# Three of seven products issued 512 columns wide, with the halves added on VectorE and v normalised on ScalarE

## The reference, cut to what matters

```python
def _spatial_gating_mixer(h, w_in, ln_g, ln_b, w_s, b_s, w_out):
    bsz, s, _ = h.shape
    proj = h @ w_in                                  # 1024 -> 3 x 2048
    z = proj[..., :E_WIDTH]
    uv = jax.nn.gelu(proj[..., E_WIDTH:], approximate=False)
    u, v = jnp.split(uv, 2, axis=-1)
    v = _layernorm(v, ln_g, ln_b)
    vc = v.reshape(bsz, s // CHUNK, CHUNK, SG_HEADS, SG_HEAD_DIM)
    sv = jnp.einsum('gpq,bnqge->bnpge', w_s, vc) + b_s.T[None, None, :, :, None]
    y = u * sv.reshape(bsz, s, E_WIDTH) * jax.nn.silu(z)
    return y @ w_out
```

## Time and profile before

| What | Value |
|---|---|
| median of 3 runs | 814.75 us |
| span of the profiled execution, first to last instruction | 812.9 us |
| PE busy | 803.3 us, 99% of the span |
| DVE busy | 649.2 us, 80% |
| ACT busy | 442.6 us, 54% |
| mean granted TensorE clock | 0.998 |
| u and z stage, from its first matmul to the first of the output product | 535.86 to 712.02 us |

### The profile page before, as it was taken

One profiled execution on the slowest core, in us unless ns is written; L12 is line 12 of the kernel. 1 busy time (PEld: TensorE's weight loads), 2 busy tenths in 40 slices (PEclk: granted clock), 3 DMA queues, 4 the chain that ended last, 5 costly groups with the idle time before them and its releaser, 6 DMA issues.

```text
span 812.9 us, 15224 instructions
## 1 busy us (share of the span) xinstructions
PE 803.3 (99%) x5614; PEld 752.5 (93%) x5614; DVE 649.2 (80%) x950; ACT 442.6 (54%) x624; POOL 50.9 (6%) x68
## 2 busy tenths in 40 slices
PE   9999999999999999999999999999999999999997
PEld 8779999999999999988889888899999999988896
DVE  5989999999999999898653787567888888897534
ACT  4575656565656666562332844446667677762220
POOL 1010000000000000000000000010000000000000
PEclk9999999999999999999999999999999999999999
DMA  9994566666565656587422162414555445487103
GB/s 350 366 245 131 153 185 179 184 177 190 171 196 166 202 164 198 171 315 288 160 79 79 61 250 98 134 21 143 148 155 148 125 140 148 136 303 265 52 1 104
DMA packets 39566, 137.85 MB, mean 170 GB/s; under 512 B 4336, under 2 KB 6512, under 8 KB 39536
## 3 DMA queue, kind: packets, MB, share of 16 engines
q1 hardware_dynamic: 31616, 110.64, 37.0%
q0 software_dynamic: 6912, 25.17, 16.4%
q10 hardware_dynamic: 1008, 1.66, 0.6%
HBM read 108.09 MB, written 4.19 MB: 138 GB/s over the span
## 4 chain that ended last, share of the span: by engine, by line
PE 94%; DVE 3%; issue 2%; ACT 0%; POOL 0%; POOLq 0%; DVEq 0%; ACTq 0%
PE pp L1190 11%; PE pp L1191 11%; PE pp L1192 11%; PE pp L1046 8%; PE pp L1048 7%; PE pp L1047 7%; PE p_aux L1190 7%; PE p_aux L1192 7%; PE p_aux L1191 7%; PE pp L1328 4%; PE pp L1326 4%; PE pp L1327 4%; PE p_aux L1400 2%; PE pp L1145 1%; PE pp L1062 1%
## 5 line engine op out<-in xcount | busy, mean ns | idle before, releaser
L1190 PE MATMUL pp<-h_hi,wh 128*128 128x256 f32 x280 | 79.3, 283 | 0.0
L1192 PE MATMUL pp<-h_hi,wl 128*128 128x256 f32 x280 | 79.2, 283 | 0.0
L1191 PE MATMUL pp<-h_lo,wh 128*128 128x256 f32 x280 | 79.2, 283 | 0.0
L1701 DVE TENSOR_TENSOR wl<-wt,wh 128x1024 fp32r<-128x1024 f32 x56 | 66.5, 1219 | 0.2 <-ACT wh L698 0.2
L698 ACT ACTIVATE wh<-wt 128x1024 fp32r<-128x1024 f32 x56 | 58.9, 1054 | 13.7 <-DVE wt L1682 7.6
L1190 PE MATMUL pp<-s_hi,wh 128*128 128x256 f32 x224 | 63.4, 283 | 0.0
L1191 PE MATMUL pp<-s_lo,wh 128*128 128x256 f32 x224 | 63.4, 283 | 0.0
L1192 PE MATMUL pp<-s_hi,wl 128*128 128x256 f32 x224 | 63.4, 283 | 0.0
L1192 PE MATMUL p_aux<-s_hi,wl 128*128 128x256 f32 x224 | 63.4, 283 | 0.0
L1191 PE MATMUL p_aux<-s_lo,wh 128*128 128x256 f32 x224 | 63.4, 283 | 0.0
L1190 PE MATMUL p_aux<-s_hi,wh 128*128 128x256 f32 x224 | 63.4, 283 | 0.0
(11 more groups left out here) (237 smaller groups left out, 2598.1 us busy)
## 6 DMA issues: line engine op xcount, KB each, us to landing
raw<-in_stream SPq DMA_DIRECT2D x144, 512.0 KB, 4.0
wl<-raw POOLq DMA_DIRECT2D x28, 512.0 KB, 4.5
raw_l<-in_stream SPq DMA_DIRECT2D x18, 512.0 KB, 4.6
raw_s<-in_stream SPq DMA_DIRECT2D x16, 512.0 KB, 13.6
wl_b<-raw POOLq DMA_DIRECT2D x16, 512.0 KB, 4.5
raw_m<-in_stream SPq DMA_DIRECT2D x14, 512.0 KB, 3.2
x_s<-in_xt SPq DMA_DIRECT2D x4, 512.0 KB, 6.0
w_lo_s<-raw POOLq DMA_DIRECT2D x4, 512.0 KB, 5.4
```

What stands on the lines that cost most here:

```text
L1190: pe.matmul(out, hi, hi_of(k), start=fresh and k == 0, stop=False, skip_group_check=not fresh)
L1191: pe.matmul(out, hi, lo_of(k), start=False, stop=False, skip_group_check=not fresh)
L1192: mm = pe.matmul(out, lo, hi_of(k), start=False, stop=k == 3, skip_group_check=not fresh)
L1701: dve.tensor_tensor(wl[par][:, part], wt[par][:, part], f32(wh[par][:, part]), ALU.subtract).then_inc(t_cut, 1)
```

## The change

In Q1, Q6 and Q7 of each group the high weights are multiplied by high and low data in one matmul of 512 columns: the high half goes to the left half of bank A, the low half to the right one. The low weights times high data stay a matmul of 256 columns into the left half. For that `s_hi` with `s_lo`, and `h_hi` with `h_lo`, become one tensor each, at the addresses they had. The two halves of the bank must now be added: ScalarE copies the left half as before, and VectorE then adds the right half to the copy (`add_p`), and only this addition counts `copied_b`, on which TensorE waits. The layer norm of v moves from VectorE (`tensor_scalar`) to ScalarE (`Identity` with a scale and a bias for each partition); VectorE makes `minus_mean` once for it. The lists of both engines are put in another order.

```diff
-                act.activation(pc_b[:, g, (0, 2, 1)[n], :], bank_a_b[g][:, 0:HALF], ACT.Copy).then_inc(copied_b, 1)
+                act.activation(pc_b[:, g, (0, 2, 1)[n], :], bank_a_b[g][:, 0:HALF], ACT.Copy).then_inc(half_copied_b, 1)
+
+            def normalise(i):
+                if isinstance(i, int) and i == 0:
+                    act.wait_ge(ln_ready, 1)
+                act.wait_ge(sv_done, 2 * i + FREE)
+                for st in range(NCH):
+                    ...
+                    act.activation(vn[:, :, at_st], src, ACT.Identity, scale=ln_rstd[:, st:st + 1],
+                                   bias=minus_mean[:, st:st + 1]).then_inc(vn_cut, 1)
@@ beside_u
                 hi_t_b(i, 1, 1)
+                normalise(i)
+                copy_p_b(i, 0, 2)
                 hi_b2_b(i, 1)
-                copy_p_b(i, 0, 2)
                 neg_b2_b(1)
                 if not isinstance(i, int) or i:
                     silu_z_b(i - 1)
@@ beside_z
                 copy_p_b(i, 1, 0)
                 cut_b11_b(i + 1, 0)
+                copy_p_b(i, 1, 1)
+                hi_b2_b(i + 1, 0)
+                neg_b2_b(0)
                 hi_t_b(i + 1, 0, 0)
-                copy_p_b(i, 1, 1)
                 hi_t_b(i + 1, 0, 1)
-                hi_b2_b(i + 1, 0)
                 copy_p_b(i, 1, 2)
-                neg_b2_b(0)
                 gelu_u(i)
@@ tensor
+            def wide_product(bank, at, width, par, both_of, fresh):
+                for k in range(4):
+                    hi, lo = (a[par][:, at + width * k:at + width * k + P] for a in (wh_b, wl_b))
+                    both = both_of(k)
+                    def high(start):
+                        return pe.matmul(bank.rearrange("p (a e) -> p a e", e=HALF), hi, both, start=start, stop=k == 3,
+                                         skip_group_check=True)
+                    if k == 0:
+                        high(fresh)
+                    mm = pe.matmul(bank[:, 0:HALF], lo, both[:, 0, :], start=False, stop=False, skip_group_check=True)
+                    if k:
+                        mm = high(False)
+                mm.then_inc(prod_b, 1)
@@ vector
+            dve.scalar_tensor_tensor(out=minus_mean[:, :], in0=mv[:, :, 0], scalar=-1.0, in1=ln_rstd[:, :],
+                                     op0=ALU.mult, op1=ALU.mult).then_inc(ln_ready, 1)
+            def add_p(i, g, n):
+                part = pc_b[:, g, (0, 2, 1)[n], :]
+                dve.wait_ge(half_copied_b, of_b(i, g, 3, n + 1))
+                dve.tensor_tensor(part, part, bank_a_b[g][:, halves[1]], ALU.add).then_inc(copied_b, 1)
@@ while_u
+                    t_sums_b(i, 1)
+                add_p(i, 0, 0)
                 if later:
-                    t_sums_b(i, 1)
                     b11_low_b(i, 1)
                     c_12_b(i - 1, 1)
-                    mixed(i - 1)
+                    mixed(i - 1, (i, 0, 1))
+                else:
+                    add_p(i, 0, 1)
                 t_low_b(i, 1, 0)
                 if later:
                     times_u(i - 1)
-                t_low_b(i, 1, 1)
+                add_p(i, 0, 2)
                 if later:
                     after(at[0])
                 c_22_b(i, 0)
-                normalise(i)
+                t_low_b(i, 1, 1)
@@ while_z
+                add_p(i, 1, 0)
                 c_first_b(i, 0)
+                c_12_b(i, 0)
+                add_p(i, 1, 1)
                 t_sums_b(i + 1, 0)
                 b11_low_b(i + 1, 0)
-                c_12_b(i, 0)
                 if not isinstance(i, int) or i > 0:
                     times_z(i - 1, at[0])
-                t_low_b(i + 1, 0, 0)
-                t_low_b(i + 1, 0, 1)
+                add_p(i, 1, 2)
                 ...
                 c_22_b(i, 1)
+                t_low_b(i + 1, 0, 0)
+                t_low_b(i + 1, 0, 1)
```

More of the change, by code:

```diff
@@ L175, in build @@
         wt = [at_kb(f"wt{par}", 28 * par + 14, [P, 2048]) for par in range(2)]
-        s_hi = at_kb("s_hi", 92, [P, 4, 4, HALF], F32R)
-        s_lo = at_kb("s_lo", 108, [P, 4, 4, HALF], F32R)
+        s_both = at_kb("s_both", 92, [P, 2, 4, 4, HALF], F32R)
+        s_hi, s_lo = (s_both[:, n, :, :, :] for n in range(2))
         s_f = at_kb("s_f", 108, [P, 4, 4, HALF])
@@ L203, in build @@
         term = at_kb("term", 196, [P, 2, P])
-        h_hi = at_kb("h_hi", 60, [P, KD, S], F32R)
-        h_lo = at_kb("h_lo", 76, [P, KD, S], F32R)
+        h_both = at_kb("h_both", 60, [P, 2, KD, S], F32R)
+        h_hi, h_lo = (h_both[:, n, :, :] for n in range(2))
         raw = at_kb("raw", 156, [P, RING, SLOT])
@@ L220, in build @@
         mv = sb("mv", [P, NCH, 2])
+        minus_mean = sb("minus_mean", [P, NCH])
         ident = sb("ident", [P, P])
@@ L285, in build @@
         b11_hi_b, b11_cut_b, b2_in_b = sem("b11_hi_b"), sem("b11_cut_b"), [sem(f"b2_in_b{g}") for g in range(2)]
+        ln_ready, half_copied_b = sem("ln_ready"), sem("half_copied_b")
         neg_b, lo_begun_b = sem("neg_b"), sem("lo_begun_b")
@@ L602, in _ @@
             act.sem_inc(copied, OFF)
-            act.sem_inc(copied_b, OFF)
             def cut_hi(w, slot, land, first=False, to=w_hi):
@@ L933, in copy_p_b @@
                 act.wait_ge(c_sum_b, of_b(i, g, 3, OFF - 3))
-                act.activation(pc_b[:, g, (0, 2, 1)[n], :], bank_a_b[g][:, 0:HALF], ACT.Copy).then_inc(copied_b, 1)
+                act.activation(pc_b[:, g, (0, 2, 1)[n], :], bank_a_b[g][:, 0:HALF], ACT.Copy).then_inc(half_copied_b, 1)
[4 more added lines that the diff above has]
+                for st in range(NCH):
+                    at_st = slice(P * st, P * (st + 1))
+                    src = y32[:, 2 * i:2 * i + 2, at_st] if isinstance(i, int) else y32[:, bass.ds(2 * i, 2), at_st]
+                    act.activation(vn[:, :, at_st], src, ACT.Identity, scale=ln_rstd[:, st:st + 1],
+                                   bias=minus_mean[:, st:st + 1]).then_inc(vn_cut, 1)
             def gelu_u(i):
@@ L1364, in uq1 @@
                 pe.wait_ge(copied_b, of_b(i, g, 3, OFF - 3))
-                product(bank_a_b[g][:, left], B_11, P, g, *own(0, 0), True, 1)
+                wide_product(bank_a_b[g][:, :], B_11, P, g, lambda k: h_both[:, :, k, left], True)
             def uq5(i, g):
@@ L1375, in uq6 @@
                 pe.wait_ge(copied_b, of_b(i, g, 3, OFF + 1))
-                product(bank_a_b[g][:, left], 1024, P, g, *summed(S2), False, 1)
+                wide_product(bank_a_b[g][:, :], 1024, P, g, lambda k: s_both[:, :, S2, k, :], False)
             def uq7(i, g):
                 pe.wait_ge(copied_b, of_b(i, g, 3, OFF + 2))
-                product(bank_a_b[g][:, left], 512, P, g, *summed(S3), False, 1)
+                wide_product(bank_a_b[g][:, :], 512, P, g, lambda k: s_both[:, :, S3, k, :], False)
             def uq2(i, g):
@@ L1441, in _ @@
             dve.sem_inc(c_sum_b, OFF)
+            dve.sem_inc(copied_b, OFF)
             at = [0]
@@ L2103, in _, with mixed @@
             after(step(dve.tensor_copy(ln_rstd[:, :], rstd[:, :])))
+            dve.scalar_tensor_tensor(out=minus_mean[:, :], in0=mv[:, :, 0], scalar=-1.0, in1=ln_rstd[:, :],
+                                     op0=ALU.mult, op1=ALU.mult).then_inc(ln_ready, 1)
             dve.wait_ge(bs_in, 16)
             dve.wait_ge(sv_used, 2)
[L2108 to L2116, removed]
+            def add_p(i, g, n):
+                part = pc_b[:, g, (0, 2, 1)[n], :]
+                dve.wait_ge(half_copied_b, of_b(i, g, 3, n + 1))
+                dve.tensor_tensor(part, part, bank_a_b[g][:, halves[1]], ALU.add).then_inc(copied_b, 1)
+            def mixed(i, between=None):
                 n = []
@@ L2132, in mixed @@
                                              op0=ALU.mult, op1=ALU.add).then_inc(sv_used, 1)
+                    if u == 0 and between is not None:
+                        add_p(*between)
             def times_u(i):
@@ L2184, in _ @@
             dve.sem_inc(x_updated, 1)
+            add_p(last, 1, 0)
             c_first_b(last, 0)
             c_12_b(last, 0)
+            add_p(last, 1, 1)
             times_z(last - 1, at[0])
@@ L2190, in _ @@
             y_low(PAIRS, PAIRS + 2)
+            add_p(last, 1, 2)
             dve.wait_ge(y_made_b, last)
```

## The result

The changed kernel takes 835.49 us (median of 5 runs, 835.15 to 835.91), the kernel before 814.78 (814.71 to 814.98 for the first three, up to 815.23 for all 5): ratio 1.0253, 95% interval 1.0241 to 1.0264, 20.7 us slower. The forecast was 833.7.

What follows compares the result with a forecast made beforehand. TensorE, 94% of the chain, was taken as the bound. Step 0's 4.2, seven steps' 13.5 and step 1's 0.3 give +18.0; with 1 for the clock, 812.9 becomes 831.9, plus 1.85 around it 833.7 us; range 828 to 840.

Steps and rivals of the forecast that it cites:

- TensorE's saving: Joining pairs of 256-column matmuls into 512 saves 0.0133 us a pair, 0.32 a step, 2.56 us over 192 pairs.
- Stall at Q6 of z: TensorE waits 1.97 us there in steps 1 to 7 for copy, then addition; 0.10 of it was there before.
- `hi_b2_b` 0.95: On ScalarE `hi_b2_b` now stands behind copy 3 of u, putting 0.95 us more in the chain to Q6 of z.
- the layer norm 0.40: Four `Identity` take 2.0 us against 1.65 us of room less 0.05, so ScalarE's copy 3 is 0.40 us late.
- `Identity` 0.50: Each layer-norm `Identity` of 256 columns on ScalarE takes 0.50 us start to start; four take 2.0 us.
- The addition's part: Ahead of Q6 of z, VectorE's `add_p` takes 0.42 us plus 0.04 for the gap after ScalarE's copy.
- Stall at Q6 of u: VectorE's list from Q6 of z reaches its addition late, so TensorE waits 0.38 us in each step.
- Step 1's extra 0.3: Step 1 waits another 0.3 us at Q6 of u, as its VectorE list starts late.
- Step 0: First `add_p` stands behind the layer-norm statistics on VectorE: TensorE stalls 4.07 us at Q6 of u; whole step +4.2.
- cheap layer norm: Rival: `Identity` costs like a copy and fits ScalarE's 1.65 us room; +14.4, 829.2 us, chance 0.15.
- extra table load: Rival: `Identity` isn't in gelu's table, adding 1.29 us to the chain in 7 steps; 842.8 us, chance 0.05.
- lower clock between the stalls of 2 us: Rival: each step's 2 us idle drops TensorE's clock, about 1 us a step more; 841 us, chance 0.08.

Runs made afterwards that it cites:

- the last two runs: Changed kernel with its queues reordered, 814.08 us; and the kernel before with only ScalarE's copy of Q1 of z ahead of table load and silus, 814.47 us.
- the run on the kernel before: The kernel before with one line moved: on ScalarE `hi_b2_b` behind the copy of Q7 of u instead of ahead of it; 821.54 us, ratio 1.0081.

## Why the prediction was right, point by point

By the profiled executions the difference is 833.3 - 812.9 = 20.4 us:

| part | forecast | measured |
|---|---|---|
| stage's start to mix 0 (step 0, clock) | 4.2 + 1 | 18.45 - 12.96 = 5.5 |
| mix 0 to mix 7 (7 periods) | 13.5 + 0.3 | 167.33 - 154.22 = 13.1 |
| behind mix 7, to the stage's end | 0 | 0.1 |
| before the stage | 0 | 1.0 |
| behind the stage | 0 | 0.7 |

- **TensorE's saving**: 0.053 us a product forecast, 0.04 measured. The sum took the price of a 512-wide matmul from a stream of its own kind; between 256-wide ones it stands about 0.235 from the next, not 0.227. So 1.9 us, not 2.56. The Trainium skill's 2.5 ns beyond the columns ("TensorE: Matmul & The Clock Gate", "Wait — 56ns, not 53.3ns?") would give, as an estimate, 24 x 2.5 = 60 ns a step. The 0.24 us between the last two runs is four times that, so the row was the better guide.
- **Stall at Q6 of z**: 1.97 forecast, 1.89 measured. Its parts agree too: `hi_b2_b` 0.95 (0.95 by the run on the kernel before), the layer norm 0.40 (0.34 by its move), `Identity` 0.50 (0.49 by its rows). The addition's part was taken out by no run of its own. By the rows it is as forecast: the copy ends at 624.72 + 0.36 = 625.08, and Q6 starts at 625.59 and is followed 0.10 late.
- **Stall at Q6 of u**: 0.38 forecast, 0.33 measured; it grew to 0.74 when the other stall went, as one of two waits in series does. Step 1's extra 0.3 did not come: 0.36 there.
- **Step 0**: 4.07 forecast, 4.05 measured. The clock fell, as the forecast held possible; 1.7 us of work by the windows, against 1 taken. The forecast also had 0.18 at Q3 of u and 0.29 at Q6 of z; the slow matmuls cover both in the changed kernel, and at the full clock they are 0.17 and 0.28. So the clock's own price in step 0 is 1.1 us. That the forecast put in 1 was a guess between bounds and came out well by luck.
- **Rivals**: no cheap layer norm (0.49 each), no extra table load, no lower clock between the stalls of 2 us (granted clock 1.00 from 560 to 730). That TensorE stays the bound needs copy 1 of z early. One moved line takes that stall away, but the two others keep the time at 824.38 us.
- **What was missed**: 1.7 us outside the stage, which the forecast had at nothing. Behind it, TensorE is idle 0.84 us ahead of the first product with `acc_b`, 0.21 before; that is the same 0.6 as between the last two runs. VectorE works without idle time up to `acc_b`. It has six additions more in a step and four layer-norm instructions less, but that these make it late was not tested. Before the stage, the start moves from 535.86 to 536.90. The forecast looked only at the stage, and two things lie ahead of it. In all nine profiles of the wide kernels VectorE stands idle for 0.52 or 0.53 us at 33 us, among the instructions that make `acc_s`, and in none of the three others. TensorE's eight products with `acc_s` start at 37.95 behind it, 37.49 before; why VectorE waits there stays open. And in six of the nine the granted clock falls to half at 39 for 3.4 us, behind 1.2 us of idle time and those eight matmuls of one column. The stage starts at 536.80 to 537.08 in these six and at 536.14 to 536.39 in the other three, so this costs some 0.65 us. Windows of TensorE (us, PE busy, PEclk, DMA share, GB/s) in the changed kernel, and in the run with step 0's additions early:

```profile
39.00:42.00 3.00, 3.00 (x9) 0.51 0.99 179
```
```profile
39.00:42.00 3.00, 3.00 (x14) 1.00 0.99 176
```

- **Wrong at no price**: the forecast argued that stalls of 2 us are too short for the clock to fall, since it had seen it fall in a longer gap. The clock did stay at 1.00 between them, but the reason doesn't hold: at 39 it fell behind a shorter idle time. Nor do SyncE's loads always arrive some 15 us ahead. In five of the profiles VectorE waits for one in step 1, by 0.25 to 2.56 us, though not in that of the changed kernel.

The total came within 1.8 us partly since errors cancelled: the steps cost 0.7 less than forecast; step 0 cost 0.3 more, what lay outside the stage 1.7 and its end 0.1 more. The remaining 0.4 is the time around the span, 2.0 us in the profiled execution and not 1.85, and the median's distance from that execution.

## What to carry to other kernels

An engine's busy share says nothing about where it can be late. When an operand gets a second stop (a copy, then an addition), add up the queue ahead of each stop and compare it with what the consumer does in that time; here 0.95 us of one instruction's place cost more than three times the whole saving. Joining matmuls saves a fixed part of some 10 ns a pair and not columns; price it first, for a gain of 2 us pays for no new wait at all. And removing the largest wait shows the next one, so count what is second.

## What the runs showed of the hardware that was not expected

- In step 0 of the changed kernel TensorE's granted clock read 1.00 while it was idle (540 to 543) and about half in the 3.4 us after it had resumed: the low clock mostly hits the work behind the stall. At the end of the program it fell while TensorE was idle.
- The granted clock fell to half at 39 us, behind 1.2 us of idle time and eight matmuls of one column, in six of nine profiles, and never between the stalls of 1.64 us idle in each step. The code there is the same in all nine, and the fall costs about 0.65 us.
- A matmul of 128 columns of plain fp32 takes 0.22 us and leaves two records (60 for 30 in 6.86 us, in the run with 30 dummy matmuls), where one of 256 columns of fp32r takes 0.120.
- Matmuls of 512 columns stand 0.227 us apart among themselves and about 0.235 between those of 256; the first behind a wait is followed 0.34 later (625.59 and 625.93).
